# One convolution channel group on GpSimd, the last expert added by one-hot matmuls, and modulation columns made on chip

## The chip, the cores and the metric
The kernel runs on one core of a Trainium2 chip. The metric is the time of one execution in microseconds of the device, the median of several runs.

## What is computed
Two layers with shared weights over 384 tokens (128 context tokens, 256 latent tokens) of width 1024, all in float32.
```python
def trunk_layer(x, mod, n1, n2, w_in, ..., rope=None, ctx_kv=None):
    sh1, sc1, g1, sh2, sc2, g2 = [mod[:, i][:, None, :] for i in range(6)]
    h = rms_norm(x, n1) * (1.0 + sc1) + sh1
    proj = h @ w_in
    q, k, v, u = jnp.split(proj, [Q_W, Q_W + KV_W, Q_W + 2 * KV_W], axis=-1)
    ...
    attn = block_attention(q, k_all, v_all)
    conv = conv_module(u, dw_w, dw_b, ln_g, ln_b)   # 31 taps over 512 channels, depthwise
    x = x + g1 * (jnp.concatenate([attn, conv], axis=-1) @ w_out)
    h2 = rms_norm(x, n2) * (1.0 + sc2) + sh2
    x = x + g2 * grouped_moe(h2, ...)               # 16 experts, 2 for a token
    return x, k, v
```
The six modulation vectors of a layer are silu(c) @ w_mod + b_mod, one set for context and one for latent tokens.

## The kernel before
The tokens are three tiles of 128 rows, tile 0 the context, tiles 1 and 2 latent. Everything is written out by hand: each engine has its own instruction list and semaphores order them. SyncE (SP) issues the weight loads, each 2 MB into one of eight slots of a ring, in the order of use, as soon as the slot's last user is done.

**Columns.** Norm 1 is folded into transposes: TensorE (PE) multiplies x, as stationary, by a diagonal of the row factors (L1397, `scr` and `big` are SBUF areas, `ps` is PSUM), and ACT (L731) and DVE (L952) scale and shift the transposed tiles with per-channel columns `modcol` while copying them to `hT`. `vector` (L1343) makes a modulation vector by 16 matmuls; DVE's `mod_take` (L914, L923) adds the bias and multiplies by the norm's gain; `columns` (L388) writes the rows to DRAM and reads them back as columns. In layer 0 ACT issues this between its first work and the transposed tiles, in layer 1 POOL does it early in the expert stage. Vector 2 of layer 1 is computed right after the experts of layer 0.

**Convolution.** After the projections (L1327) the gated input is transposed to channels on partitions, `zT`, 4 groups of 128 channels. DVE applies tap after tap, for the 4 groups in turn (`tap`, L996 for the first, L1000 for the others: a scalar_tensor_tensor over 128 context or 256 latent columns, both tensor operands in SBUF). The 31 context taps come first. Of the 31 latent taps 6 lie around the rotary work of the three tiles (`rope`, L1031 to L1065), 4 late ones after it, and 3 in each of the first seven heads of the attention. In rope, POOL makes the norm factors (L543 to L546) from DVE's sums (L1031), and DVE waits for them at L1034. PE interleaves quarters of vector 3 with the transposes of the roped tiles (L1451). In each head PE does transposes (L1486) and scores (L1462), a piece of vector 4 (L1357) and the product with v; DVE does maxima (L1081), 3 taps and the output (L1089). In head 3 DVE also takes half of vector 4 (L918, L923) and needs `gainB`, which POOL loads (L564).

**Experts.** POOL gathers the token rows of a pair of experts (L604), PE transposes them (L1602), and per expert come gate and up (L1618), ACT's sigmoid (L873), two DVE products (L1299, L1301), two transposes (L1627), a DVE copy (L1305), and the down projection (L1634), which is issued one expert late: down of e - 1 after gate/up of e. More than 64 tokens for an expert are an overflow, run in a loop of its own. ACT copies each result (`take_y`, L840) and stores it to `expert_rows` in DRAM (L843). After the last store POOL gathers the two result rows of every token (L650), ACT scales one (L705), and DVE combines (`combine`, L933, L934, L935) into x. Layer 1 starts from there with the square sums (L709), POOL's factor (L514, L515) and the diagonal (L944).

The order of the loads at an expert stage's end, from the list `loads`:
```python
    for e in range(1, E):
        experts += [("g", l, e), ("u", l, e), ("d", l, e - 1)]
    return items, experts + [("d", l, E - 1)]
```


## Time and profile before
| | before |
|---|---|
| median of 3 runs | 1169.36 us (1165.12 to 1169.71) |
| profiled execution, its time | 1165.68 us |
| its span | 1163.8 us |
| PE busy, DVE, ACT, POOL | 980.0, 407.9, 158.2, 116.8 us |
| granted TensorE clock, mean | 0.92 of full speed |
| DMA | 331.71 MB, mean 285 GB/s |

Times in the trace run from the span's start. A busy PE is not PE at its peak. Every float32 matmul stands in the trace as two PE instructions. The profile's shares are averages over stages: what a change is worth is read where its instructions stand, from what waits last there.

### The profile page before, as it was taken

What the parts mean: (1) busy time and instruction counts of PE and PEld (TensorE: products, weight loads), DVE (VectorE), ACT (ScalarE), POOL (GpSimd) and SP (SyncE); (2) the same over time, 40 slices, a digit from 0 to 9 for tenths busy, and PEclk for the clock granted to TensorE, in tenths of its full rate; (3) what the DMA queues carried; (4) which work ended last, traced back from release to release, by engine and by line L of the source; (5) the groups of instructions that cost most, each with busy time, mean ns of one, the idle gap of its engine ahead of it and who ended that gap; (6) DMA issues with size and microseconds to landing.
All of it is one profiled execution on the core that took longest, in us unless ns stands there. A gap on an engine that the chain in (4) does not pass through costs nothing.

```text
span 1163.8 us, 11201 instructions
## 1 busy us (share of the span) xinstructions
PE 980.0 (84%) x4106; PEld 443.5 (38%) x4106; DVE 407.9 (35%) x1072; ACT 158.2 (14%) x362; POOL 116.8 (10%) x164
## 2 busy tenths in 40 slices
PE   3589979999889988997839996999858997978890
PEld 0344525545333333333225553554523333333330
DVE  0019868733411111111042986954421111111113
ACT  0110123311000000000021023431100000000001
POOL 0100310230110000000030030041010000000001
PEclk8789979998989999998869997999769999998996
DMA  9934992348999987999975434034965999999805
GB/s 315 378 135 144 218 387 116 145 127 305 425 412 422 422 367 261 396 426 425 411 296 185 144 139 192 8 139 162 346 249 207 409 426 424 425 419 426 372 19 180
DMA packets 65412, 331.71 MB, mean 285 GB/s; under 512 B 6993, under 2 KB 9713, under 8 KB 48929
## 3 DMA queue, kind: packets, MB, share of 16 engines
q1 hardware_dynamic: 44224, 277.89, 59.9%
q10 hardware_dynamic: 12464, 23.79, 6.9%
q0 software_dynamic: 8624, 28.71, 6.8%
q8 instruction: 62, 1.02, 0.4%
q14 instruction: 38, 0.30, 0.1%
HBM read 308.25 MB, written 22.12 MB: 284 GB/s over the span
## 4 chain that ended last, share of the span: by engine, by line
PE 64%; DMA 19%; DVE 10%; issue 2%; ACT 2%; SPq 2%; POOL 1%; ACTq 0%; DVEq 0%; POOLq 0%
PE ps L1618 19%; PE ps L1327 15%; DMA big<-in_w_up_dram 10%; PE ps L1634 9%; PE ps L1534 7%; DVE scr L1000 4%; PE ps L1343 4%; DMA x<-in_x_sample_dram 2%; DMA big<-in_w_down_dram 2%; PE ps L1462 2%; DMA scr<-h_rows,slot_tok 1%; PE ps L1397 1%; DMA scr<-expert_rows,pick_y 1%; PE ps L1357 1%; PE ps L1602 1%
## 5 line engine op out<-in xcount | busy, mean ns | idle before, releaser
L1618 PE MATMUL ps<-big 128*64 128x512 f32 x1024 | 246.9, 633 | 41.3 <-DMA big<-in_w_up_dram 23.1
L1000 DVE SCALAR_TENSOR_TENSOR scr<-scr,convw 128x128 f32<-128x128 f32 (+1 forms) x480 | 160.5, 408 | 0.0
L1618 PEld LDWEIGHTS ps<-big 128*64 128x64 f32 x1024 | 82.0, 145 | 181.5 <-issue 167.4
L1634 PE MATMUL ps<-big,scr 128*64 128x512 f32 x624 | 146.3, 605 | 5.0 <-DVE scr L1290 4.3
L1327 PE MATMUL ps<-big 128*128 128x512 f32 (+1 forms) x384 | 146.1, 541 | 0.0
L1299 DVE TENSOR_TENSOR scr<-ps,scr 128x256 f32<-128x256 f32 x32 | 13.6, 425 | 309.9 <-ACT scr L873 309.9
L1343 PE MATMUL ps<-big,cs_rep 128*64 128x512 f32 x320 | 83.3, 667 | 22.0 <-DMA big<-in_w_mod_dram 22.0
L1327 PEld LDWEIGHTS ps<-big 128*128 128x128 f32 x384 | 72.9, 191 | 69.8 <-issue 67.5
L1534 PE MATMUL ps<-big 128*128 128x512 f32 x192 | 84.4, 594 | 1.4 <-ACT big L739 1.4
L1634 PEld LDWEIGHTS ps<-big,scr 128*64 128x64 f32 x624 | 49.8, 139 | 88.8 <-issue 88.3
L873 ACT ACTIVATE scr<-ps 128x256 f32<-128x256 f32 x32 | 12.3, 384 | 356.6 <-PE ps L1618 356.6
L1618 PE MATMUL ps<-big,scr 128*64 128x512 f32 x224 | 51.3, 612 | 5.9 <-DVE scr L1279 5.9
L1534 PEld LDWEIGHTS ps<-big 128*128 128x128 f32 x192 | 35.7, 190 | 43.0 <-issue 41.1
L1343 PEld LDWEIGHTS ps<-big,cs_rep 128*64 128x64 f32 x320 | 23.5, 152 | 70.4 <-issue 51.6
L1397 PE MATMUL ps<-big,x 128*128 128x128 f32 x96 | 23.8, 427 | 31.2 <-DVE big L944 21.6
L604 POOL DMA_INDIRECT scr<-h_rows,slot_tok x16 | 15.5, 969 | 288.2 <-PE ps L1602 244.3
L1462 PE MATMUL ps<-scr 64*128 64x384 f32 (+1 forms) x96 | 39.4, 500 | 0.0
L1270 DVE COPY big<-ps 128x512 f32<-128x512 f32 x32 | 20.6, 686 | 50.5 <-PE ps L1602 50.5
L1397 PEld LDWEIGHTS ps<-big,x 128*128 128x128 f32 x96 | 23.2, 335 | 33.1 <-issue 33.1
L1486 PE MATMUL ps<-table_sb,scr 128*128 128x128 f32 x112 | 22.9, 307 | 15.0 <-ACT scr L795 15.0
L1357 PE MATMUL ps<-big,cs_rep 128*2 128x512 f32 x64 | 33.4, 649 | 0.0
L1327 PEld LDWEIGHTS ps<-scr 128*128 128x128 f32 x224 | 26.9, 196 | 16.0 <-issue 13.8
(198 smaller groups left out, 758.3 us busy)
## 6 DMA issues: line engine op xcount, KB each, us to landing
big<-in_w_gate_dram SPq DMA_DIRECT2D x32, 2048.0 KB, 15.5
big<-in_w_up_dram SPq DMA_DIRECT2D x32, 2048.0 KB, 20.6
big<-in_w_down_dram SPq DMA_DIRECT2D x32, 2048.0 KB, 18.0
big<-in_w_mod_dram SPq DMA_DIRECT2D x23, 2048.0 KB, 17.5
big<-in_w_in_dram SPq DMA_DIRECT2D x6, 2048.0 KB, 28.6
expert_rows<-scr ACTq DMA_DIRECT2D x78, 128.0 KB, 8.0
big<-in_w_out_dram SPq DMA_DIRECT2D x4, 2048.0 KB, 17.4
expert_rows<-x ACTq DMA_DIRECT2D x1, 6656.0 KB, 36.4
```

Of the source, the lines that this page charges most:

```text
L604: pool.indirect_dma_start(out=xs[:, i % 2, :], out_offset=None, in_=h2_dram, in_offset=bass.IndirectOffsetOnAxis(ap=slot_tok[:, i * NT:i * ...
L1000: v.scalar_tensor_tensor(out, span, w, out, ALU.mult, ALU.add).then_inc(conv_step[part_], 1)
L1270: ins = v.tensor_copy(hT[i % 2][:, 4 * b:4 * b + 4, :].rearrange("p k n -> p (k n)"), ps[:, XT + b, :])
L1327: mm = pe.matmul(out, stationary(k), moving(k), start=(k == 0), stop=(k == n - 1))
L1343: mm = pe.matmul(ps[lane * LP:(lane + 1) * LP, mod_bank(l, j), :], cs_rep[:, k, :], w[:, lane * LW:(lane + 1) * LW], start=(k == 0), stop= ...
L1357: mm = pe.matmul(ps[0:2, mod_bank(l, c), :], cs_rep[:, k, 0:2], slot_k(slot_of(n), b - a)[:, k - a, (c - 8) * SEG:(c - 7) * SEG], start=(k ...
L1397: mm = pe.matmul(ps[:, n % 4, m * P:(m + 1) * P], x[:, t, 4 * (n % 2) + m::KD], diag[:, t, :], start=True, stop=True)
L1462: pe.matmul(ps[:, 4 + t, 0:P * len(ks)], qT[g_ * HD:(g_ + 1) * HD, t, j * P:(j + 1) * P], kT[g_ * HD:(g_ + 1) * HD, ks[0] * P:(ks[-1] + 1) ...
L1486: mm = pe.transpose(ps[:, 1 + t, n * P:(n + 1) * P], prob[:, t, n * P:(n + 1) * P], ident)
L1534: mm = pe.matmul(ps[:, out_bank(t, n), :], hT[t][:, k, :], slot_w(s)[:, k, :], start=(k == 0), stop=(k == KD - 1))
L1618: mm = pe.matmul(ps[b * TT:(b + 1) * TT, bank, :].rearrange("p (m n) -> p m n", m=2), tokens(k), w[:, :, k, b * HF:(b + 1) * HF], start=(k ...
L1634: mm = pe.matmul(ps[b * TT:(b + 1) * TT, bank, :], src[:, k % 2 * P + k // 2 * TT:k % 2 * P + (k // 2 + 1) * TT], w[:, k, b * SEG:(b + 1) ...
```

## The change
It has three parts.

1. The convolution's last group of 128 channels goes to POOL, as a product and a sum per tap (the product buffers lie in `sg`); DVE keeps 3 groups. POOL does all 31 context taps before its first norm factor of rope, 3 latent taps before the second, 3 before the third, 6 after it, and 19 after the gate's round trip and before the load of `gainB`. PE's `conv_back` waits for both.
2. The columns are made on chip: rows go from PSUM to SBUF unchanged, 16 matmuls with `ident` turn each into 64 by 2 pieces, and DVE adds bias and gain that were loaded as columns. The start's loads put x before the second vector; x is transposed between the vectors for two tiles and after the first two projections for the third. The two broadcasts of the layer norm's parameters are issued later. Vector 2 of layer 1 moves behind that layer's projections.
3. Expert 15 is not stored and gathered. DVE makes marks of token against slot, weighted; PE transposes them and ACT keeps them. In the last expert, down of 14 and the overflow come ahead of gate/up. After down of 15, 6 matmuls of 64 rows spread its rows to tokens in PSUM, and DVE adds them (`add_last`) after the picked rows (`add_picked`). The gather waits for the stores up to expert 14.

```diff
+DVE_CM, POOL_M = CM - 1, CM - 1
+POOL_TAPS = [3, 3, 6]
-        items = vec[4:6] + proj + vec[6:10] + out + vec[10:12]
+        items = proj + vec[4:10] + out + vec[10:12]
...
             load_vector(0, 0)
-            load_vector(0, 1)
             sp.dma_start(x[:, 0, :], x_prompt[0]).then_inc(x_in, 16)
             sp.dma_start(x[:, 1:3, :], x_sample[0].rearrange("(t p) n -> p t n", p=P)).then_inc(x_in, 16)
+            load_vector(0, 1)
             for l in range(LAYERS):
-                if l:
-                    load_vector(l, 2)
...
+                    for k in range(k0, k0 + n):
+                        span = zT[:, POOL_M, k + o0:k + o0 + w_]
+                        w = convw[:, POOL_M, k:k + 1]
+                        product = sg[:, k % 2 * 2 * P:k % 2 * 2 * P + w_]
...
+                            done = l * (2 * TAPS) + part_ * TAPS + k
+                            pool.wait_ge(pool_conv, done - 1)
+                            g.tensor_scalar(product, span, w, None, ALU.mult).then_inc(pool_mul, 1)
+                            pool.wait_ge(pool_conv, done)
+                            pool.wait_ge(pool_mul, l * (2 * TAPS - 2) + part_ * (TAPS - 1) + k)
+                            g.tensor_tensor(out, out, product, ALU.add).then_inc(pool_conv, 1)
...
+                taps(0, 0, TAPS)
+                for t in range(TILES):
+                    if t == 1:
+                        pool.wait_ge(zT_ready, l * 3 + 3)
+                    if t:
+                        taps(1, sum(POOL_TAPS[:t - 1]), POOL_TAPS[t - 1])
                     pool.wait_ge(qk_ss, l * 3 + t + 1)
...
+                taps(1, sum(POOL_TAPS[:2]), POOL_TAPS[2])
                 pool.wait_ge(mod_taken, taken_at(l, 2))
                 lane_out(pool, mod_dram[:, 2 * D:3 * D], rowC, modC_st)
...
+                taps(1, sum(POOL_TAPS), TAPS - sum(POOL_TAPS))
                 pool.wait_ge(slot_used[slot_of(("in", l, 3))], uses(("in", l, 3)))
                 pool.dma_start(gainB, norm2_g[l:l + 1, :].broadcast_to([2, D])).then_inc(gain_in, 16)
...
                 for b in range(2):
-                    pool.wait_ge(y_st[b], (l + 1) * (E * 16))
+                    pool.wait_ge(y_st[b], (l + 1) * ((E // 2 - b) * 32))
...
+                soon = 1 if l + 1 < LAYERS else TILES
+                for t in range(soon):
+                    scale_pick(l, t)
                 take_y(E - 1)
-            for t in range(TILES):
-                scale_pick(LAYERS - 1, t)
+                for t in range(soon, TILES):
+                    scale_pick(l, t)
...
+            def add_last(l, t):
+
+                a1 = pick_buf[t][1]
+                dve.wait_ge(fin_ps, l * TILES + t + 1)
+                step.link(v.tensor_tensor(a1, ps[:, 2 * FIN[t]:2 * FIN[t] + 2, :].rearrange("p b n -> p (b n)"),
+                                          gateB[:, group(t), :], ALU.mult))
+                v.tensor_tensor(x[:, t, :], x[:, t, :], a1, ALU.add).then_inc(combined, 1)
...
                 if l:
-                    mod_take(l, 2)
-                    combine(l - 1, 0)
-                    combine(l - 1, 1)
+                    add_picked(l - 1, 0)
+                    add_last(l - 1, 0)
+                    columns(l)
+                    add_picked(l - 1, 1)
                     scale_tile(0)
-                    combine(l - 1, 2)
+                    add_last(l - 1, 1)
+                    add_picked(l - 1, 2)
+                    add_last(l - 1, 2)
...
+            def columns(l, s_):
+
+                pe.wait_ge(mod_taken, taken_at(l, s_))
+                for k in range(KD):
+                    for b in range(LANES):
+                        mm = pe.matmul(ps[b * LP:(b + 1) * LP, col_bank(l, s_), 2 * (s_ * KD + k):2 * (s_ * KD + k) + 2],
+                                       rowA[:, s_ * LW + k:(s_ + 1) * LW:KD], ident[:, b * LP:b * LP + 2],
+                                       start=True, stop=True)
+                mm.then_inc(cols_ps, 1)
...
+                    if e == E - 1:
+                        down_main(e - 1)
                     loaded(("g", l, e))
                     loaded(("u", l, e))
+                    if e == E - 1:
+                        overflow(pe, n, run, ov_at)
                     gate_up(GU, e, lambda k: hT[i % 2][:, k, j * TT:(j + 1) * TT]).then_inc(gu_ps, 1)
...
                 down_main(E - 1)
+                pe.wait_ge(y_taken, (l + 1) * E)
+                for t in range(TILES):
+                    for b in range(2):
+                        mm = pe.matmul(ps[:, 2 * FIN[t] + b, :], last_T[b * TT:(b + 1) * TT, t, :],
+                                       ybuf[b * TT:(b + 1) * TT, 1, :], start=True, stop=True)
+                    mm.then_inc(fin_ps, 1)
```

The order on POOL around rope, before (L543 to L546 are the norm factors of a tile, L551 and L553 the cache outputs, L292 to L285 the gate's way through DRAM, L564 the gain):
```order
L540 MEMSET scr 128x4x15
L543 TENSOR_SCALAR stat<-stat 128x8
...
L551 DMA out_dram<-scr 128x128
L553 DMA out_dram<-scr 128x128
L543 TENSOR_SCALAR stat<-stat 128x8
L544 TENSOR_SCALAR stat<-stat 128x2
L546 TENSOR_TENSOR stat<-stat 128x10
...
L519 DMA gateB<-mod_rows 128x2x1024
L285 DMA rowC<-in_b_mod_dram 64x512 x2
L564 DMA big<-in_norm_g_dram 2x1024
```
And now, from the cache outputs on (L559 is a product, L562 a sum, L574 to L577 the norm factors):
```order
L582 DMA out_dram<-scr 128x128
L584 DMA out_dram<-scr 128x128
L554 TENSOR_SCALAR scr<-scr,convw 128x256
L559 TENSOR_SCALAR scr<-scr,convw 128x256
L562 TENSOR_TENSOR scr<-scr 128x256
L559 TENSOR_SCALAR scr<-scr,convw 128x256
L562 TENSOR_TENSOR scr<-scr 128x256
L574 TENSOR_SCALAR stat<-stat 128x8
L575 TENSOR_SCALAR stat<-stat 128x2
L577 TENSOR_TENSOR stat<-stat 128x10
```
Between the outputs for the cache and the second tile's factors there now stand five operations on 256 columns; ahead of the first tile's stand 61 on 128.

The order on PE from the last down projection of layer 0 to the projections of layer 1, before:
```order
L1618 MATMUL ps<-big 64x512 x16
L1634 MATMUL ps<-big,scr 64x512 x8
L1627 MATMUL ps<-table_sb,scr 128x128 x2
...
L1648 MATMUL ps<-table_sb 1x1 x2
L1634 MATMUL ps<-big,scr 64x512 x8
L1343 MATMUL ps<-big,cs_rep 64x512 x16
L1397 MATMUL ps<-big,x 128x128 x24
L1327 MATMUL ps<-big 128x512 x24
```
And now (L1727 gate/up, L1743 down, L1830 the one-hot matmuls, L1462 the columns, L1472 the transposes of x, L1419 the projections):
```order
L1727 MATMUL ps<-big 64x512 x16
L1736 MATMUL ps<-table_sb,scr 128x128 x2
L1759 MATMUL ps<-table_sb 1x1 x2
L1743 MATMUL ps<-big,scr 64x512 x8
L1830 MATMUL ps<-scr 128x512 x6
L1462 MATMUL ps<-table_sb,scr 64x2 x32
L1472 MATMUL ps<-big,x 128x128 x16
L1419 MATMUL ps<-big 128x512 x16
L1472 MATMUL ps<-big,x 128x128 x8
L1419 MATMUL ps<-big 128x512 x8
```
The down projection of expert 14 has left its place between gate/up and down of 15, vector 2 (L1343) is gone from here, and two groups stand between the last down projection and the transposes of x.

## Rows read from the trace of the kernel before

**Rows 1.** Page, chain that ended last, shares by engine:
```profile
PE 64%; DMA 19%; DVE 10%; issue 2%; ACT 2%; SPq 2%; POOL 1%; ACTq 0%; DVEq 0%; POOLq 0%
```
**Rows 2.** Chain in order of time, the start: start us, us, what:
```profile
17.38 23.91 DMA x<-in_x_sample_dram
...
59.79 1.52 ACT big L731 x4
...
65.56 21.34 PE ps L1327 x48
```
**Rows 3.** Timeline of DVE in heads 1 and 2 (start, us, what, idle before):
```profile
181.39 4.83 DVE L1000 SCALAR_TENSOR_TENSOR scr<-scr,convw 128x256 f32<-128x256 f32 x12
...
187.59 0.56 DVE L1081 TENSOR_REDUCE stat<-ps 128x1 f32<-128x384 f32 x1 [0.23 <-PE ps L1462]
188.07 4.83 DVE L1000 SCALAR_TENSOR_TENSOR scr<-scr,convw 128x256 f32<-128x256 f32 x12
```
**Rows 4.** Timeline at the end of layer 0's experts, and windows, DMA GB/s last:
```profile
560.40 9.48 PE L1618 MATMUL ps<-big 128*64 128x512 f32 x32 [4.07 <-DMA big<-in_w_up_dram]
...
574.27 3.65 PE L1634 MATMUL ps<-big,scr 128*64 128x512 f32 x16 [0.35 <-DVE scr L1305]
...
560.00:565.00 5.00, 4.60 (x12) 1.65 (x14) 0.00 (x0) 0.00 (x0) 0.00 (x0) 0.50 1.01 421
```
**Rows 5.** Timeline from the experts of layer 0 to the projections of layer 1:
```profile
594.37 1.15 ACT L705 ACTIVATE scr<-scr,gates 128x1024 f32<-128x1024 f32 x1 [15.75 <-DMA scr<-expert_rows,pick_y]
...
604.37 11.72 PE L1397 MATMUL ps<-big,x 128*128 128x128 f32 x48 [19.07 <-DVE big L944]
...
615.92 1.45 PE L1327 MATMUL ps<-big 128*128 128x512 f32 x3
```
**Rows 6.** Timeline of the program's end:
```profile
1118.48 7.09 PE L1618 MATMUL ps<-big,scr 128*64 128x512 f32 x32 [0.78 <-DVE scr L1279]
...
1128.09 5.35 PE L1634 MATMUL ps<-big,scr 128*64 128x512 f32 x16 [0.61 <-DVE scr L1290]
...
1148.21 1.15 ACT L705 ACTIVATE scr<-scr,gates 128x1024 f32<-128x1024 f32 x1 [10.33 <-DMA scr<-expert_rows,pick_y]
...
1159.52 1.23 DVE L935 TENSOR_TENSOR x<-x,scr 128x1024 f32<-128x1024 f32 x1
```
**Rows 7.** Timeline of PE, last group of vector 3 in layer 0:
```profile
155.15 1.94 PE L1343 MATMUL ps<-big,cs_rep 128*64 128x512 f32 x8
```
**Rows 8.** Groups of POOL by form: busy us, mean ns, idle before:
```profile
L575 POOL TENSOR_TENSOR big<-big,lnB 128x512 f32<-128x512 f32 x6 | 7.6, 1263 | 5.5 <-DVE big L1102 5.5
...
L539 POOL MEMSET scr<- 128x120 f32 x2 | 0.5, 234 | 0.0
```
**Rows 9.** Timelines where DVE and POOL meet with SBUF operands:
```profile
240.45 1.28 POOL L580 TENSOR_TENSOR big<-big,scr 128x512 f32<-128x512 f32 x1 [0.80 <-ACT scr L818]
...
240.99 1.28 DVE L1138 TENSOR_TENSOR x<-x,scr 128x512 f32<-128x512 f32 x1
...
604.47 1.00 POOL L514 TENSOR_SCALAR stat<-stat 128x1 f32<-128x1 f32 x1 [0.57 <-ACT big L709]
...
609.20 0.19 POOL L514 TENSOR_SCALAR stat<-stat 128x1 f32<-128x1 f32 x1 [2.12 <-ACT big L709]
...
244.76 0.69 DVE L1138 TENSOR_TENSOR x<-x,scr 128x512 f32<-128x512 f32 x1
```
**Rows 10.** Timeline of rope in layer 0, small POOL operations beside taps:
```profile
124.55 1.65 DVE L1000 SCALAR_TENSOR_TENSOR scr<-scr,convw 128x256 f32<-128x256 f32 x4
...
125.55 2.11 POOL L546 TENSOR_TENSOR stat<-stat 128x10 f32<-128x10 f32 x1
```
**Rows 11.** Timelines of rope: POOL in layer 0, DVE's last step, PE in layer 1:
```profile
132.52 0.35 POOL L543 TENSOR_SCALAR stat<-stat 128x8 f32<-128x8 f32 x1 [1.52 <-DVE stat L1031]
...
149.90 0.28 DVE L1065 TENSOR_TENSOR scr<-scr 128x128 f32<-128x128 f32 x1
...
690.00 1.94 PE L1343 MATMUL ps<-big,cs_rep 128*64 128x512 f32 x8
...
699.41 0.28 DVE L1065 TENSOR_TENSOR scr<-scr 128x128 f32<-128x128 f32 x1
```

More of the change, by code:

```diff
@@ L171, in mod_bank, with col_bank @@
     if j == 2:
-        return 1 if l == 0 else 4
+        return 1
     return {3: 0, 8: 0, 9: 0, 5: 3}[j]
+def col_bank(l, s):
+    return 5 if l else 6 + s
+FIN = [0, 1, 3]
 def taken_at(l, j):
@@ L439, in _ @@
                     load(("in", l, m), w_in_v[l, :, :, c0:c0 + n], n)
-                for j in (2, 3, 4) if l == 0 else (3, 4):
+                for j in (2, 3, 4):
                     load_vector(l, j)
@@ L834, in take_y @@
                 def take_y(k):
[L836 removed]
+                    j = k % 2
+                    before = l * (E // 2 - j) + k // 2
                     if past(before):
@@ L975, in _ @@
                     mod_take(0, 1)
+                    columns(0)
+                dve.wait_ge(cols_ready, l + 1)
                 for t in range(TILES):
@@ L1296, in run @@
                         more_hidT()
+                    if e == E - 1:
+                        overflow(dve, n, run, ov_at)
                     dve.wait_ge(sig_ready, l * E + e + 1)
@@ L1363, in head_fill, with x_transposed @@
                             mm.then_inc(slot_used[slot_of(n)], 1)
+            def columns(l, s_):
[6 more added lines that the diff above has]
+                mm.then_inc(cols_ps, 1)
+            def x_transposed(l, t):
+                pe.wait_ge(diag_ready, l * 3 + t + 1)
+                for n in range(2 * t, 2 * t + 2):
+                    for m in range(4):
+                        mm = pe.matmul(ps[:, n % 4, m * P:(m + 1) * P], x[:, t, 4 * (n % 2) + m::KD], diag[:, t, :],
+                                       start=True, stop=True)
+                    mm.then_inc(hT_ps, 1)
             vector(0, 0)
-            vector(0, 1)
             pe.wait_ge(table_in, 16)
             pe.wait_ge(router_in, 32)
+            columns(0, 0)
+            x_transposed(0, 0)
+            x_transposed(0, 1)
+            vector(0, 1)
+            columns(0, 1)
             for l in range(LAYERS):
                 if l:
-                    vector(l, 2)
-                    pe.wait_ge(y_taken, l * E)
+                    columns(l, 0)
+                    columns(l, 1)
+                    x_transposed(l, 0)
+                    x_transposed(l, 1)
                 def transposed(t):
```

167 lines of the change are left out of this document (104 added, 63 removed).

## The prediction
> **What bounds the kernel now.** I read the page's chain of waits first, then the timeline of each stretch that the change touches, then the by-form groups for prices. The chain is mostly TensorE, with DVE in second place among the engines [rows 1]: what counts is whether a piece lies where TensorE waits. Four places matter.
>
> *The start.* x lands at 17.38 + 23.91 = 41.3 us, ACT applies the columns, after a round trip of the rows through DRAM, only at 59.79, and the first projection starts at 65.56 [rows 2]. *The attention stretch.* In heads 1 to 3 one DVE tap group follows another every 188.07 - 181.39 = 6.68 us, and DVE waits for PE in between, 0.23 before one of its reductions [rows 3]. So a head takes PE 6.68 us, and taking taps off DVE shortens no head; only the four late taps before head 0 stand alone on the path. *The end of layer 0.* PE waited for the last up-weights until 560.3, then came gate/up of expert 15 and down of 14, and down of 15 from 574.27 to 577.9 [rows 4]; the picked rows were there only at 594.37 and projections began at 615.92 [rows 5]. *The end of the program.* From the last down projection's copy to the picked rows 10.33 us, then three combines until 1159.52 + 1.23 = 1160.75 [rows 6].
>
> **Part 1, the start: gain 10.9 us.** The 9.5 MB before x's landing are the same; now the last to land is the last quarter of the second vector, at 41.3. Its 8 PE instructions take 2.7 us (0.33 each, between the 0.24 and the half-clock 0.43; an instruction of that kind is 1.94/8 = 0.24 [rows 7]), the DVE copy 0.8, which gives 44.8. Then the columns: 16 matmuls are 32 instructions, since each float32 matmul shows as two. Their stationary is strided like x's in the x transposes, which cost 11.72/48 = 0.244 each with 128 columns [rows 5]; with 64 columns I take half, 0.122, so 3.9 us (bounds: a quarter to all of 0.244, 2.0 to 7.8). Two small DVE operations, 0.5, and four activations, 1.5 [rows 2], give the first projection at 50.8, 14.8 earlier. The transposes of tile 2 are moved, not removed: they now stand between projections and cost 16 x 0.244 = 3.9. So 10.9 gained, between 7.0 and 12.8.
>
> **Part 2, the convolution's fourth channel group on POOL.** Removed from DVE per layer: 31 prompt and 31 sample operations. Added to POOL: 61 operations on 128 columns and 61 on 256 (a product and a sum for each tap, one for the first). POOL prices: a two-input sum of 512 columns is 1.263 [rows 8], one of almost no columns 0.19 [rows 9], so 2.1 ns a column: 0.73 for 256, 0.46 for 128. A one-input product of that width does not occur; it costs at least the 0.234 of a 120-column memset [rows 8] and at most the sum's 0.73. I take 0.45, in the middle. With 0.12 between operations a sample tap is 1.3 us (1.1 to 1.6), a prompt tap 0.88.
> The Trainium skill (GPSIMD Engine Reference, Performance versus the Vector engine) has 2.6 cycles an element for two inputs and (When to use GPSIMD) one-input operations near line rate; by it a product of 256 would be about 0.40 us, an estimate, and the sum would move by under 1 us. The same section says to leave elementwise work to the Vector engine.
>
> *The two engines block each other.* At 240.99 a DVE add of two SBUF operands, 0.69 elsewhere, took 1.28 because a POOL sum had begun at 240.45: it ended 0.54 after POOL's end, the time of its own data. At 604.47 a POOL operation of 0.19 took 1.00, until DVE's ended [rows 9]. A tap on DVE has two SBUF inputs too. POOL gets in between two back-to-back taps: at 124.55 four taps kept their pace, 1.65, while tiny POOL operations passed [rows 10]. So I let them alternate: one POOL operation, one DVE tap. A sample tap of POOL then takes 1.6 us and lets through 2 DVE taps, 0.8 each in place of 4.83/12 = 0.40 [rows 3].
> The Trainium skill (SBUF — State Buffer, Who interferes with whom) says whoever starts first holds the pair for the whole instruction. The POOL operation of 2.11 us with 10 columns left the DVE taps alone [rows 10], against the letter of that: I charge the reading time only. By the page's wording a DVE tap under POOL would be 1.0 us, and the total about 4 us more.
>
> Prompt taps: POOL needs 31 x 1.0 = 31 us blocked, DVE does 93 operations in about the 33 us that 124 took. No change. *Rope:* POOL now has 3 taps between its first and second norm. POOL has issued the cache DMAs at 132.52 - 1.52 = 131.0 and began the second norm at 132.5 [rows 11]; three taps of 1.3 and a little blocking last until 135.3: +2.8. Rope of tile 1, 4.4 us of two-input operations, meets 3 more taps: +2.0, minus 0.4 for the missing channel and the 0.4 that DVE waited: +4.0. Rope of tile 2 meets the 6 taps: +3.5. It ended at 150.18 in layer 0 and 699.69 in layer 1 [rows 11]; now 7.5 later. In layer 0 PE came to it 5 us after it was ready (its last vector group began at 155.15 [rows 7]), so +3.1 remain. In layer 1 PE waited for it, so all 7.5 count. *Late taps:* 12 for 16, -1.6. *Heads:* POOL has 19 taps left after the gate's DMA round trip. It starts them about 169, and between then and head 1's taps DVE is mostly idle; there 7 to 8 cost nothing. The other 11 to 12 fall on heads 1 and 2, where DVE's 9 taps take 7.2 at full alternation and the head 8.8 in place of 6.68: +2.1, and +1.4 in the second: +3.5. Nothing comes back in later heads, PE's 6.68 hold. Layer 0: 3.1 - 1.6 + 3.5 + 0.2 = +5.2. Layer 1: 7.5 - 1.6 + 3.5 = +9.4.
> *Queued behind POOL's taps:* the load of norm2's gain. DVE asks for it in head 3, at about 204 in this timeline; POOL is done by 192. Cover of 10 us.
>
> **Part 3, vector 2 of layer 1** moves out of the gap after the experts to behind the projections: 32 instructions of 0.22 (7.09/32, [rows 6]), 7.1 us. I cost it at nothing: PE would be ready for the last rope at 690.0 + 7.1 + 1.9 + two groups of 2.6 = 704.2 [rows 11], and the rope, covering it, is ready at 707.2. If rope is not late, 4 us. The PE wait of 3 us brings its low clock: 560.40 shows 9.48 for 32 instructions after a wait of 4.07 where 0.22 each is usual [rows 4, 6]. +1.0.
>
> **Part 4, expert 15 by one-hot matmuls, end of layer 0: loss 7.1 us.** Down of expert 14 must now come first, but its weights land after the up-weights of 15 (2 MB at 421 GB/s are 5.0 us [rows 4]): 565.3. Down 14 at part-low clock until 571.3, gate/up 15 until 578.5, its sigmoid and products are no longer covered (2.5, as between 1118.48 + 7.09 and 1128.09 [rows 6]), down 15 until 584.7 (before: 577.9). Row 14's copy ends at 571.9; at the 15.75 us that copy to picked row took [rows 5] the rows are there at 587.7. ACT scales tile 0 first, 1.15, then copies expert 15, 0.6: 589.5. 12 final PE instructions of 512 columns, 4.0 at half to full clock, then 64 column instructions, 7.8: 601.3. DVE waits for them with its list: columns 0.6, then 3.85 + 0.3 + 2.5 + 3.85 + 2.5 + 0.3 to the diagonal of tile 1, at 615.2 (operations of 1.23 [rows 6] and the gaps). Transposes 3.9 give the first projection at 619.1, with tile 2's 3.9 still to come: 623.0 against 615.92. Bounds: columns at 0.06 and 0.244 each, +2 to +15.
>
> **Part 5.** Nine more small DVE operations before the experts, 2 us, mostly behind the gather: +0.5. *End of program:* the picked rows come while PE does expert 15, so the three combines start about 1137.6 rather than 1149.5 (1148.21 and ACT's scaling), but they grow from 3.76 to 3.85 + 2.5 each; and expert 15's chain is 1.2 longer (2.5 uncovered, against 1.3 of the slow 5.35 down [rows 6]). Tile 2 is done at 1156.7, not 1160.75 [rows 6]: -4.0.
>
> **Sum:** -10.9 + 5.2 + 7.1 + 9.4 + 1.0 + 0.5 - 4.0 = +8.3, on the profiled execution's 1165.68: 1174.0. That run lies 3.7 below the median shown, 1169.36. I add half of it, 1.8: **1176 us**, slower by 0.6%.
>
> **Rivals.**
> *A. The block costs little* (POOL slips into DVE's bubbles, products are short). For: tiny POOL operations did not slow taps [rows 10]. Against: both 512-column cases were blocked in full. Layer 0 gains 1.9, layer 1 loses 2.4 (vector 2 is then exposed): -10.9 - 1.9 + 7.1 + 2.4 + 0.5 - 4.0 = -6.8, on the same base 1161: faster.
> *B. POOL becomes the bound.* At over 1.9 us a blocked tap the 19 taps are not done when DVE asks for the gain in head 3, and everything behind stands. At 2.3 us: 8 us a layer there and 3 more in rope: 1176 + 22 = 1198. For: rope and taps of DVE block POOL too [rows 9]; against: the prices above leave 10 us.
> *C. The chip-made columns of layer 1 are dear:* PE at low clock through final and column matmuls, 0.244 each: +8, 1184.
> *D. The change does not unload DVE in effect but the start and the end pay as computed and layer 0's end costs only its lower bound:* 1171, no change.
>
> **Chances.** My forecast 0.52, of which 0.24 slower, 0.23 within, 0.05 faster, since its terms sit near the line of 0.5% (5.8 us, about what a measurement of this kernel tells from no change). A 0.27 (0.25 faster), B 0.11, C 0.05, D 0.05. Faster 0.30, same 0.27, slower 0.43. Range 1156 to 1196: from A with the start's best bound to B nearly whole.
>
> **What would show it.** The first projection near 51 us. DVE taps of 256 columns at 0.7 to 0.9 wherever POOL taps run, 0.40 else; POOL sums of 0.73 stretched to about 1.0. Rope of tile 2 ending 7 us later relative to the projections; heads 1 and 2 near 8.8 us, heads 4 to 7 at 6.68. At layer 0's end: down 14 waiting for weights, DVE waiting for the columns about 7 us. I am wrong if taps keep 0.40 beside POOL taps, if a head past 2 still waits for POOL, or if the projections of layer 1 begin no later than before relative to the last up-weights.

## The result, and the profile after

The changed kernel takes **1192.1 us** (median of 4 runs, 1183.5 to 1193.8) where the kernel before takes 1167.2 (median of 4 beside it): **ratio 1.020, 95% interval 1.017 to 1.024**, slower by 24.9 us. The forecast was 1176 us, slower by 0.6%. The direction was as forecast and the time lies in the range of 1156 to 1196; the loss is three times the 8.3 us that the sum gave, and not the forecast case came but rival B, in which POOL becomes the bound. The profiled execution of the changed kernel took 1190.67 us, its span 1188.8.

The table is read from the traces: when TensorE begins or ends each stage in the two profiled executions, and the lead (-) or lag (+) of the changed kernel. The filler matmuls are the piece of vector 4 in a head (L1357 before, L1449 now); "convolution transposed back" is the start of the transposes that bring the convolution's result back behind the last head.

| place (TensorE) | before | after | after - before |
|---|---|---|---|
| first projection of layer 0 | 65.4 | 46.7 | -18.7 |
| its projections done | 140.6 | 126.6 | -14.0 |
| filler matmuls of head 0 | 172.3 | 164.4 | -7.9 |
| convolution transposed back | 222.2 | 224.2 | +2.0 |
| first gate/up | 316.4 | 317.9 | +1.5 |
| last down projection's weights land | 570.8 | 577.0 | +6.2 |
| layer 1's projections done | 690.1 | 699.0 | +9.0 |
| filler matmuls of head 0 | 717.6 | 737.2 | +19.7 |
| convolution transposed back | 767.9 | 797.1 | +29.3 |
| last down projection's weights land | 1105.0 | 1129.6 | +24.6 |
| end of the span | 1163.8 | 1188.8 | +25.0 |

The losses stand between "projections done" and "convolution transposed back", 16.0 us in layer 0 and 20.3 in layer 1. The chain of waits, which had 1% of POOL [rows 1], now goes through POOL's taps. The page, shares by engine (this chain goes back no further than 706.84 us, so its shares add up to 40%):

```profile
PE 23%; DMA 7%; POOL 4%; DVE 3%; issue 2%; ACT 1%; ACTq 0%; DVEq 0%; SPq 0%; POOLq 0%
```

*The start.* The timeline of TensorE in the changed kernel (start, us, then engine, line, operation, tiles, shape, count, and in brackets the idle time before and what ended it), to be held against [rows 2]:

```profile
34.71 7.09 PE L1435 MATMUL ps<-big,cs_rep 128*64 128x512 f32 x32
42.59 2.09 PE L1462 MATMUL ps<-table_sb,scr 128*64 128x2 f32 x32 [0.79 <-DVE scr L958]
46.70 15.70 PE L1419 MATMUL ps<-big 128*128 128x512 f32 x32 [2.02 <-ACT big L762]
62.23 3.84 PE L1472 MATMUL ps<-big,x 128*128 128x128 f32 x16
```

The 32 column instructions take 2.09 us, 0.065 each; the first projection starts at 46.70, and tile 2's transposes (3.84) stand between projections as computed.

*POOL's prices.* Groups of the changed kernel by form (busy us, mean ns, idle before); before, only a sum of 512 columns and tiny operations were to be seen [rows 8]:

```profile
L559 POOL TENSOR_SCALAR scr<-scr,convw 128x256 f32<-128x256 f32 x60 | 67.7, 1129 | 0.1
L562 POOL TENSOR_TENSOR scr<-scr 128x256 f32<-128x256 f32 x60 | 44.3, 738 | 9.2 <-POOL scr L559 0.8
L559 POOL TENSOR_SCALAR scr<-scr,convw 128x128 f32<-128x128 f32 x60 | 38.5, 641 | 0.0
L562 POOL TENSOR_TENSOR scr<-scr 128x128 f32<-128x128 f32 x60 | 33.8, 563 | 9.3 <-POOL scr L559 0.5
L554 POOL TENSOR_SCALAR scr<-scr,convw 128x256 f32<-128x256 f32 x2 | 1.1, 564 | 0.1
```

The sums cost what was forecast. The product (L559) is the dear half of the tap, dearer than the sum, though it reads one tensor; the first tap (L554), which multiplies and adds, takes half of it. With no tap of DVE beside it (first three rows below, timeline of POOL) one tap follows the other every 1.77 us; beside DVE's taps (the next three) 1.95. DVE's taps there (last row, timeline of DVE) take 3.97/6 = 0.66 each, where 0.40 was usual [rows 3]:

```profile
162.93 0.92 POOL L559 TENSOR_SCALAR scr<-scr,convw 128x256 f32<-128x256 f32 x1
164.00 0.72 POOL L562 TENSOR_TENSOR scr<-scr 128x256 f32<-128x256 f32 x1
164.70 0.92 POOL L559 TENSOR_SCALAR scr<-scr,convw 128x256 f32<-128x256 f32 x1
...
183.39 1.09 POOL L559 TENSOR_SCALAR scr<-scr,convw 128x256 f32<-128x256 f32 x1
184.64 0.72 POOL L562 TENSOR_TENSOR scr<-scr 128x256 f32<-128x256 f32 x1
185.34 1.10 POOL L559 TENSOR_SCALAR scr<-scr,convw 128x256 f32<-128x256 f32 x1
...
181.67 3.97 DVE L1076 SCALAR_TENSOR_TENSOR scr<-scr,convw 128x256 f32<-128x256 f32 x6
```

*Rope.* The timeline of DVE shows it waiting for POOL's norm factors three times, and its own two-input steps stretched (L1127 takes 1.23; the same step, L1051 before, took 0.82 and 0.83):

```profile
118.50 0.83 DVE L1110 TENSOR_TENSOR scr<-scr,stat 128x640 f32<-128x640 f32 x1 [7.72 <-POOL stat L577]
...
128.86 0.83 DVE L1110 TENSOR_TENSOR scr<-scr,stat 128x640 f32<-128x640 f32 x1 [5.11 <-POOL stat L577]
...
140.15 0.83 DVE L1110 TENSOR_TENSOR scr<-scr,stat 128x640 f32<-128x640 f32 x1 [1.88 <-POOL stat L577]
...
142.01 1.23 DVE L1127 TENSOR_TENSOR scr<-scr,table_sb 128x640 f32<-128x640 f32 x1
...
145.49 0.28 DVE L1141 TENSOR_TENSOR scr<-scr 128x128 f32<-128x128 f32 x1
```

The first wait, 7.72, is for POOL's 31 prompt taps: they ran from 75.00 to 115.83, 1.32 us each. Rope ends at 145.77, which is 159.7 in the timeline of before (its projections ended 14.0 later), against 150.19 [rows 11]: 9.5 later.

*The heads.* One head of each layer takes 15.6 and 14.8 us where the others take 6.7 to 8.1. In the timeline around it, DVE wants the gain at 193.1; POOL is at its taps until 196.7 and only then issues the load. The first row is the same DVE step in the kernel before, which did not wait:

```profile
200.28 0.68 DVE L923 SCALAR_TENSOR_TENSOR big<-big 2x512 f32<-2x512 f32 x1
...
192.46 0.67 DVE L966 TENSOR_TENSOR big<-ps,big 2x512 f32<-2x512 f32 x1
...
196.01 0.72 POOL L562 TENSOR_TENSOR scr<-scr 128x256 f32<-128x256 f32 x1
196.67 0.58 POOL L597 DMA_DIRECT2D big<-in_norm_g_dram  x1
198.69 0.68 DVE L971 SCALAR_TENSOR_TENSOR big<-big 2x512 f32<-2x512 f32 x1 [5.56 <-DMA big<-in_norm_g_dram]
```

TensorE falls idle behind it, and when it comes back its granted clock is low. Windows (length; busy time of PE, PEld, DVE, ACT, POOL with counts; granted clock; DMA share; GB/s):

```profile
200.00:209.00 9.00, 9.00 (x28) 5.65 (x29) 5.79 (x17) 3.83 (x13) 0.00 (x0) 0.50 0.00 0
216.00:222.00 6.00, 6.00 (x30) 2.82 (x29) 4.56 (x12) 2.95 (x10) 0.00 (x0) 1.00 0.44 177
```

After DVE's wait of 5.6 us TensorE runs the next 9 us at 0.50, the level of 1.2 GHz. The head takes 15.65 us instead of 6.68 and the next one 7.65, so the wait costs nearly twice its length.

*The end of layer 0* (timeline of TensorE; [rows 4, 5] before): down of 14 waits for weights, and the columns come before the first transposes.

```profile
572.29 5.50 PE L1743 MATMUL ps<-big,scr 128*64 128x512 f32 x16 [8.10 <-DMA big<-in_w_down_dram]
577.61 7.05 PE L1727 MATMUL ps<-big 128*64 128x512 f32 x32
...
587.07 3.65 PE L1743 MATMUL ps<-big,scr 128*64 128x512 f32 x16 [0.35 <-DVE scr L1394]
594.31 5.49 PE L1830 MATMUL ps<-scr 64*128 64x512 f32 x12 [3.59 <-ACT scr L875]
599.73 4.01 PE L1462 MATMUL ps<-table_sb,scr 128*64 128x2 f32 x64
```

### The profile page after: what moved, and what is told of

The parts are those of the page before. It is cut to its first block and busy times, and to the rows that moved or that the text cites. A ratio compares the mean times of both kernels' runs of the same rounds, so it can differ in the third digit from the quotient of the medians.

```text
span 1188.8 us, 11788 instructions
## 1 busy us (share of the span) xinstructions
PE 1013.0 (85%) x4264; PEld 464.4 (39%) x4264; DVE 419.7 (35%) x982; ACT 158.8 (13%) x364; POOL 297.0 (25%) x404
## 5 line engine op out<-in xcount | busy, mean ns | idle before, releaser
L1727 PE MATMUL ps<-big 128*64 128x512 f32 x1024 | 243.0, 625 | 31.4 <-issue 12.3
L1743 PE MATMUL ps<-big,scr 128*64 128x512 f32 x624 | 151.4, 624 | 13.1 <-DMA big<-in_w_down_dram 8.1
L1076 DVE SCALAR_TENSOR_TENSOR scr<-scr,convw 128x128 f32<-128x128 f32 (+1 forms) x360 | 150.4, 488 | 0.0
L1419 PE MATMUL ps<-big 128*128 128x512 f32 (+1 forms) x384 | 147.4, 544 | 2.0 <-ACT big L762 2.0
L1727 PEld LDWEIGHTS ps<-big 128*64 128x64 f32 x1024 | 80.7, 143 | 168.9 <-issue 156.7
L559 POOL TENSOR_SCALAR scr<-scr,convw 128x128 f32<-128x128 f32 (+1 forms) x120 | 106.2, 885 | 0.1
L1419 PEld LDWEIGHTS ps<-big 128*128 128x128 f32 x384 | 73.0, 192 | 71.6 <-issue 67.1
L639 POOL DMA_INDIRECT scr<-h_rows,slot_tok x16 | 15.4, 964 | 311.3 <-PE ps L1711 265.0
L1743 PEld LDWEIGHTS ps<-big,scr 128*64 128x64 f32 x624 | 51.2, 143 | 99.7 <-issue 97.6
L562 POOL TENSOR_TENSOR scr<-scr 128x128 f32<-128x128 f32 (+1 forms) x120 | 78.0, 650 | 18.5 <-POOL scr L559 1.3
L1727 PE MATMUL ps<-big,scr 128*64 128x512 f32 x224 | 51.3, 612 | 5.9 <-DVE scr L1366 5.9
L1570 PE MATMUL ps<-scr 64*128 64x384 f32 (+1 forms) x96 | 42.9, 539 | 0.0
L659 POOL DMA_INDIRECT scr<-h_rows,slot_tok x7 | 6.6, 948 | 131.3 <-PE ps L1727 126.2
L1419 PE MATMUL ps<-scr 128*128 128x64 f32 x224 | 31.3, 297 | 8.8 <-DVE big L1164 8.8
L1419 PEld LDWEIGHTS ps<-scr 128*128 128x128 f32 x224 | 29.0, 209 | 24.1 <-issue 13.5
L1357 DVE COPY big<-ps 128x512 f32<-128x512 f32 x32 | 20.6, 686 | 46.4 <-PE ps L1711 46.4
## 6 DMA issues: line engine op xcount, KB each, us to landing
big<-in_w_gate_dram SPq DMA_DIRECT2D x32, 2048.0 KB, 14.6
big<-in_w_up_dram SPq DMA_DIRECT2D x32, 2048.0 KB, 20.3
```

What stands on the lines that cost most here:

```text
L559: g.tensor_scalar(product, span, w, None, ALU.mult).then_inc(pool_mul, 1)
L562: g.tensor_tensor(out, out, product, ALU.add).then_inc(pool_conv, 1)
L639: pool.indirect_dma_start(out=xs[:, i % 2, :], out_offset=None, in_=h2_dram, in_offset=bass.IndirectOffsetOnAxis(ap=slot_tok[:, i * NT:i * ...
L1076: v.scalar_tensor_tensor(out, span, w, out, ALU.mult, ALU.add).then_inc(conv_step[part_], 1)
L1357: ins = v.tensor_copy(hT[i % 2][:, 4 * b:4 * b + 4, :].rearrange("p k n -> p (k n)"), ps[:, XT + b, :])
L1419: mm = pe.matmul(out, stationary(k), moving(k), start=(k == 0), stop=(k == n - 1))
```

## The experiments

Ten runs of nine kernels follow (e11 is e5's kernel again); "e" names are labels. All ratios are to the kernel before, each to the executions of it that ran beside. My theory after reading the traces was a queue: POOL's taps hold back what stands behind them (norm factors, the gain load). The rival was the port: DVE and POOL slow each other wherever the taps stand.

**e1, the gain load ahead of the taps.**
```diff
-                taps(1, sum(POOL_TAPS), TAPS - sum(POOL_TAPS))
                 pool.wait_ge(slot_used[slot_of(("in", l, 3))], uses(("in", l, 3)))
                 pool.dma_start(gainB, norm2_g[l:l + 1, :].broadcast_to([2, D])).then_inc(gain_in, 16)
+                taps(1, sum(POOL_TAPS), TAPS - sum(POOL_TAPS))
```


> The load of norm2's gain is issued ahead of POOL's last 19 taps instead of behind them. Theory (the queue): in the changed kernel one head of each layer takes 15.6 us instead of 6.7 because DVE waits for that gain, which sits behind POOL's taps. With the load ahead, all heads from the third on take 6.7 us, each layer's attention ends about 9.8 us sooner, and the whole is 1172 us (-19.6). Rival (the port): it is the DVE and POOL taps blocking each other that makes the heads long; then the heads stay long and the whole moves by less than 4 us.

Measured 1176.8 us (ratio 1.010, 1.008 to 1.012): 15.3 us below the changed kernel. The waits of DVE in layer 0's heads no longer have the gain among them; the changed kernel's first, then e1's (total, times, longest):
```profile
DVE big L971 <- DMA big<-in_norm_g_dram: 5.6, 1, 5.6
```
```profile
DVE stat L1156 <- PE ps L1570: 9.4, 9, 2.1
DVE stat L1162 <- PE ps L1419: 6.4, 2, 6.1
DVE big L966 <- PE ps L1449: 1.5, 1, 1.5
```
From projections done to the convolution transposed back, layer 1 is 9.5 us shorter, as expected. Layer 0 is only 4.5 shorter: there TensorE did heads 0 and 1 at the low clock for longer (12.4 and 8.2 us, where the changed kernel took 7.7 and 6.7; granted clock 0.50 to 0.51 from 160 to 180, where the changed kernel had 0.86 from 165 to 170 and then 1.00). That is not the edit's doing: one execution of e5's kernel has the same slow heads (12.4 and 8.1), another of the same kernel, in e11, has 9.0 and 6.7. So some 5 us of this stretch change from execution to execution, and the profiled one of e1 had them. The queue theory holds; the port rival does not explain the long head.

**e2, the whole convolution on DVE.**
```diff
-DVE_CM, POOL_M = CM - 1, CM - 1
+DVE_CM = CM
...
-                taps(0, 0, TAPS)
...
-                        pe.wait_ge(pool_conv, (l + 1) * (2 * TAPS))
```


> The fourth channel group of the convolution goes back to DVE; the columns made on chip, vector 2 behind the projections and the one-hot matmuls stay, and the gain load stays where it is in the program (nothing long is ahead of it now). Theory: the whole of the loss in the attention stretch comes from POOL's taps: the gain wait 2 x 9.8, the later rope and the late taps 6.1 in layer 0 and about 6.5 in layer 1 (vector 2, 7.1 us of PE, then stands partly uncovered): 1160 us, below the kernel before. Rival: the taps on POOL cost only the wait for the gain, and taking a channel group off DVE is otherwise worth its price: then the time equals that of the run with the load ahead, about 1172 us.

Measured 1162.6 us (ratio 0.996, 0.994 to 0.998): in this kernel all POOL taps together cost 29.5 us, and without them the change is slightly faster than the kernel before. From projections done to the convolution transposed back: 81.8 in each layer; before 81.6 and 77.8, after 97.6 and 98.1. So POOL's group costs 16 us in each layer. The 4.0 that layer 1 keeps is vector 2, no longer covered.

**e3, no POOL taps between the norms of rope** (on e1).
```diff
-POOL_TAPS = [3, 3, 6]
+POOL_TAPS = [0, 0, 12]
```


> As the run with the gain load ahead, and in addition POOL does none of its sample taps between the three norms of rope: 12 stand behind the third norm instead of 3, 3 and 6. Theory (POOL holds the norm factors back behind its taps): rope of tile 2 ends about 7 us sooner in each layer; 4 us of that reach the heads in layer 0, and 4 in layer 1, where vector 2 then limits: 8 us below the run with the gain load ahead, about 1164 us. Rival (port): rope is slow because POOL's taps run beside it wherever they stand; then the late taps and rope just trade places and the time is within 3 us of that run.

Measured 1168.1 us (ratio 1.001, 0.999 to 1.004), 8.7 below e1, against 8 expected. From projections done to the first filler matmuls both layers are shorter, by 5.1 and 5.5 us. The scores of head 0 start at 144.4 instead of 149.9, and in layer 1 at 704.9 instead of 719.0 (of that, 6.5 is carried over from layer 0). Order on POOL, not only the port, made rope late. The first norm still waits, since the prompt taps still stand ahead of it:
```profile
119.83 0.82 DVE L1110 TENSOR_TENSOR scr<-scr,stat 128x640 f32<-128x640 f32 x1 [7.73 <-POOL stat L577]
```

**e4, the product in another form** (on e1).
```diff
-                            g.tensor_scalar(product, span, w, None, ALU.mult).then_inc(pool_mul, 1)
+                            g.tensor_scalar(product, span, w, zT[:, POOL_M, 0:1], ALU.mult, ALU.add).then_inc(pool_mul, 1)
```


> As the run with the gain load ahead, with the product of each POOL tap in the form of the first tap: two scalars from memory, multiply and add (the second scalar is a zero of the pad). In the changed kernel a product of 256 columns takes 0.92 us with nothing beside it, a first tap of two scalars only 0.57. If the form makes the difference, products fall to about 0.57 at 256 columns, rope of tile 2 ends 2 us sooner and the whole falls by 2 to 4 us against the run with the gain load ahead. If it is not the form (the first tap is short for another reason), the products stay at 0.92 or more and the time stays within 1.5 us.

Measured 1169.5 us (ratio 1.003, 1.001 to 1.005), 7.3 below e1: more than the 2 to 4 expected. It is the form. From projections done to the first filler matmuls layer 0 is 3.1 and layer 1 is 3.0 us shorter. The timeline of POOL with no tap of DVE beside it:
```profile
163.09 0.56 POOL L559 TENSOR_SCALAR scr<-scr,convw 128x256 f32<-128x256 f32 x1
163.80 0.72 POOL L562 TENSOR_TENSOR scr<-scr 128x256 f32<-128x256 f32 x1
164.51 0.56 POOL L559 TENSOR_SCALAR scr<-scr,convw 128x256 f32<-128x256 f32 x1
```
The same product, with a zero added, takes 0.56 instead of 0.92, and a tap 1.42 instead of 1.77.

**e5, expert 15 back to the gathered rows** (on e2).
```diff
-                    if e == E - 1:
-                        down_main(e - 1)
...
-                    if 0 < e < E - 1:
+                    if e:
                         down_main(e - 1)
...
-                        mm = pe.matmul(ps[:, 2 * FIN[t] + b, :], last_T[b * TT:(b + 1) * TT, t, :],
-                                       ybuf[b * TT:(b + 1) * TT, 1, :], start=True, stop=True)
...
-                add_last(l - 1, 0)
```


> On top of the run with the whole convolution on DVE (1162.6 us): expert 15 goes back to the gathered rows, down of 14 behind gate/up of 15, no one-hot matmuls, no marks; the columns stay on chip and now run while PE waits for the picked rows. Theory from the traces: the one-hot order costs 6.2 us at the last down projection of layer 0 and gives back about 3 by the shorter path to the first projection, and it gives about 2 us at the program's end. Undone: layer 0's last down 6 us sooner after its weights land, projections of layer 1 done 3 us sooner, program's end 2 us longer: 1161 us. Rival (the terms as forecast: 7.1 lost in layer 0, 4.0 gained at the end): 3.1 us less, 1159.5 us; second rival, that the order of the last experts makes no difference because picked rows set both ends: no change, 1162.6 within 1.5.

Measured 1155.6 us (ratio 0.989, 0.984 to 0.994), 7.0 below e2: more than either expectation; by the second measurement of the same kernel (e11, 1158.0) it is 4.6. In both kernels the last down projection's weights land at 565.6. The timeline of e2, then of e5, around that last down projection:
```profile
560.67 5.33 PE L1713 MATMUL ps<-big,scr 128*64 128x512 f32 x16 [8.28 <-DMA big<-in_w_down_dram]
565.82 7.05 PE L1697 MATMUL ps<-big 128*64 128x512 f32 x32
...
575.28 3.65 PE L1713 MATMUL ps<-big,scr 128*64 128x512 f32 x16 [0.35 <-DVE scr L1365]
```
```profile
562.54 3.62 PE L1673 MATMUL ps<-big,scr 128*64 128x512 f32 x16
...
567.11 3.65 PE L1673 MATMUL ps<-big,scr 128*64 128x512 f32 x16 [0.35 <-DVE scr L1327]
```
The reordering costs 8.2 us there, and 8.4 are left when layer 1's projections are done: nothing of it comes back. Nor does the program's end give anything in this pair: from the first gate/up of layer 1 to the end of the span e2 takes 308.1 and e5 308.3. Two other pairs below (e10, and e8 with e9) do not bear that out.

**e7, vector 2 of layer 1 back in front of the projections** (on e5).
```diff
-        items = proj + vec[4:10] + out + vec[10:12]
+        items = vec[4:6] + proj + vec[6:10] + out + vec[10:12]
...
                     columns(l, 1)
+                    vector(l, 2)
```


> As the run without one-hot matmuls, with vector 2 of layer 1 back in front of the projections, behind the columns. What is left of the change is the columns made on chip and the earlier transposes. Against the kernel before the start then gives 14 to 15 us up to the first expert. Theory: in the experts of layer 0 that lead shrinks to about 5 us, as it did in the run with the convolution on DVE, so the whole gains 5 to 7 us against before (1160 us), and against the run without one-hot matmuls vector 2 is hidden again: 2 to 4 us. Rival: the lead is kept when nothing else is changed, 1152 us.

Measured 1159.1 us (ratio 0.993, 0.989 to 0.996), near the 1160 expected, but not 2 to 4 us below e5, from which it can't be told apart. Two effects in the traces cancel. The attention stretch of layer 1 is 4.3 us shorter (76.5 against 80.8): vector 2 is covered again. But its 4 MB are now loaded while the picked rows are fetched. The row that shows the first rows arriving, in e5 and in e7, both timelines of ACT:
```profile
584.49 1.15 ACT L712 ACTIVATE big<-big,gates 128x1024 f32<-128x1024 f32 x1 [13.04 <-DMA scr<-expert_rows,pick_y]
```
```profile
584.62 1.15 ACT L715 ACTIVATE big<-big,gates 128x1024 f32<-128x1024 f32 x1 [17.15 <-DMA scr<-expert_rows,pick_y]
```
e7's last down projection ended 4 us sooner, and the rows came no sooner: 9.8 us from the gather's issue to arrival with the queues at 390 to 406 GB/s, 6.5 in e5, where they had gone down to 43 when it was issued. The start alone gives 14.6 us until the convolution is taken back (207.6 against 222.2) and about 8 in the time of the kernel.

**e8 and e9, the channel group kept on POOL with the repairs together**, e8 with the one-hot matmuls, e9 without: e1, e3 and e4 (and e5) in one.

> The change with three repairs together: the gain load ahead of POOL's last 19 taps, no POOL taps between the norms of rope, products in the two-scalar form. The three alone or in pairs gave 1168.1 and 1169.5 us. If they add up, rope of tile 2 ends as in the run with the convolution on DVE and no head waits: 1161 to 1163 us, no better than with the convolution on DVE (1162.6), since PE and not DVE sets the length of a head. Rival: freed DVE time is worth something somewhere (late taps 1.6 us a layer), then up to 3 us below the run with the convolution on DVE.

> All repairs that keep the channel group on POOL: gain load ahead, no taps between the norms, two-scalar products, and expert 15 back to the gathered rows. If the costs add, it is the 1162.5 us of the run with the three repairs less 7: 1155.5 us, equal to the run with the convolution on DVE and no one-hot matmuls. Rival: POOL's group costs a few us once nothing else hides it (vector 2 and rope limit layer 1): 1158 us or more.

Measured: e8 1162.5 us (ratio 0.996, 0.993 to 0.999), the same as e2. e9 1159.4 (0.993, 0.991 to 0.996), against 1155.6 and 1158.0 for e5's kernel: no gain over the convolution on DVE. Put right, POOL's taps cost and bring nothing that these runs can tell (e8 against e2 0.0 us; e9 against e11, measured beside it, 1.4 us with overlapping intervals), since TensorE's 6.7 us set a head. From e8 to e9 the gathered rows gave 3.1 us and not 7: layer 0's end became 7.1 shorter (from the landing of the last weights to projections done, 121.8 to 114.7), but the stretch from layer 1's first gate/up to the end 9.0 longer (302.5 to 311.5).

**e10, the changed kernel with only the one-hot order undone.**

> The changed kernel with only the one-hot order of expert 15 undone (POOL's taps, the late gain load and everything else stay). With the convolution on DVE the same edit gave 7.0 us, of which 8.4 at the end of layer 0 and nothing at the program's end. If that cost is independent of POOL's taps the changed kernel falls by 7 us to 1185. Rival: it depends on them, since in the changed kernel layer 0's experts start later and the weights may land before PE asks; then less than 3 us.

Measured 1185.9 us (ratio 1.016, 1.012 to 1.020), 6.2 below the changed kernel. That is near the 7 of independent costs, but the intervals of the two kernels overlap, as they do for e2 and e5's kernel and for e8 and e9: the one-hot order costs 3 to 7 us, the same way in all three pairs, and how it depends on POOL's taps is not resolved. In the traces layer 0's end is 4.0 shorter here (122.0 to 118.0), and from layer 1's first gate/up to the end it is 3.2 longer (305.7 to 308.9).

**e11, e5's kernel again.**

> The run with the convolution on DVE and no one-hot matmuls again, with five rounds, as the candidate that beats both kernels: 1156 us, a ratio of 0.990 to the kernel before; if the first measurement (1155.6, four runs) was lucky, up to 1159.

Measured 1158.0 us (ratio 0.993, 0.990 to 0.995). With the first measurement: 9 to 11 us faster than before, 34 to 37 than the changed kernel. No version beat it.

## Why the prediction was right and wrong

**Part 2, the price of a POOL tap: the step that failed.** "I take 0.45, in the middle" for a product of 256 columns, with 0.73 as the most: it is 0.92, above the bound. The bound leaned on a product costing "at most the sum's 0.73", and this form of product costs more than the sum. A tap was therefore 1.77 free and 1.95 blocked, not 1.3 and 1.6; e4, where the product takes 0.56, gives 7.3 us back by that alone. The price of the sum (0.73) and the direction were right. That POOL and DVE delay each other was right too, with other sizes: three DVE taps pass in one POOL tap, at 0.66 each, where I had two at 0.8. The effects below followed, and e2 measures them all at 29.5 us where my terms for the attention stretch gave 5.2 + 9.4:
- *The queue behind the taps.* "Cover of 10 us" for the gain load. In the timeline of before POOL would be done at 196.7 + 14.0 = 210.7 instead of 192, and DVE asked at 207 (forecast 204). Five us of the 18.7 between are an error of my own sum: from 169, 7.5 taps at 1.3 and 11.5 at 1.6 end at 197 and not at 192, so the cover was 7 us and not 10. The rest is mostly the price, which acts twice: the 19 taps took 35.6 us, 1.87 each, and they began only at 161.1 + 14.0 = 175.1, since the six taps ahead of the gate's round trip had taken 12.7 us. Rival B gave exactly this mechanism, from 1.9 us a blocked tap; 1.95 was measured. I put 0.11 on it and priced it at 8 us a layer; e1 measured 15.3 in all. I had not charged the 9 us at half clock behind the wait, which nearly double it.
- *"No change" for the prompt taps.* The 31 taps took 40.8 us, not 31, and DVE waited 7.72 for the first norm factor behind them.
- *Rope* ended 9.5 later in layer 0, where I had 7.5; DVE's waits for the second and third norm were as described, and e3 got back 8.7 by order alone. The slow heads 1 and 2 that I charged with 3.5 a layer did not happen: 7.7 and 6.7 us.

**Part 1, the start.** Forecast 10.9, measured 14.0 at the end of the projections. Columns cost 0.065 an instruction, near the lower bound of 0.06 that comes from a quarter of 0.244, not 0.122; whether the 2 moving or the 64 stationary columns set that is not shown. The second vector was done at 41.8, not at 44.0. What failed is the step after it: I carried the gain in full to the end of the program. In e2 the lead is 15.0 us at the first gate/up and 5.2 when layer 0's last weights land. In e5 it is 7.8 (its slow heads) and again 5.2, in e11 11.7 and 5.5. Three leads end at one landing time, 565.4 to 565.6, so it is not TensorE's start that sets it, but most likely the stream of weights; no run tests that.

**Part 3.** "At nothing" was covered only while rope was late, as the text says: with rope in order (e5 against e7) vector 2 costs 4 us in layer 1, the 4 that I had named for that case. That moving its loads away leaves the picked rows a free queue, worth about as much, was not foreseen.

**Part 4, layer 0's end.** Forecast +7.1, measured +2.8 from the landing of the last weights (9.0 - 6.2). The reordered experts came as computed: down 15 ended 590.72 - 6.2 = 584.5 in before's timeline, forecast 584.7. The columns were over-sized (4.0 against 7.8), the one-hot matmuls under-sized (5.5 against 4.0). But one-hot matmuls and on-chip columns were summed as one edit. Apart they are 8.4 lost (e2 against e5) and, with vector 2 moved away, about 5 gained: from the last weights' landing to projections done, before takes 119.3, e5 114.6.

**Part 5, the program's end.** Forecast -4.0. From the overflow part of expert 14 to the end the changed kernel is 2.9 us shorter, since 1163.8 - 1090.5 = 73.3 became 1188.8 - 1118.4 = 70.4. But from the landing of the last weights it is 58.8 before and 59.2 after. Ahead of expert 14's gate/up TensorE stood 2.7 us with nothing released that the profile shows and 1.8 us for weights, and the gate/up took 10.0 us instead of 7.1. So the term was partly right in its own stretch and brought nothing here. Whether the one-hot order pays at the end stays open: from layer 1's first gate/up to the end it is 0.2, 3.2 and 9.0 us shorter with it in the three pairs.

**The sum as a whole.** Without POOL's terms my parts give -10.9 + 7.1 + 0.5 - 4.0, and +4 for the vector 2 that then shows: -3.3. e2 came out 4.0 below the kernel before. That agreement is luck: the start was worth 5.2 and not 10.9 by layer 0's last weights, layer 0's end cost 3.7 and not 7.1, and the program's end gave nothing. Two figures do not follow from the prediction's own parts: its cases add up to 0.30 for "same" and 0.40 for "slower", not 0.27 and 0.43, and rival A with the start's best bound is 1159, not 1156.

**Not in the sum.** In all eleven profiles that start in the new way (columns on chip) TensorE stands 5.2 to 6.7 us between expert 0's gate/up and the next one in layer 0, with nothing released that the profile shows. In the kernel before it stands 0.55 there and 3.27 one expert later. The kernel before, the changed kernel, then e11, timelines of TensorE:
```profile
325.34 0.24 PE L1648 MATMUL ps<-table_sb 128*1 128x1 f32 x4
326.13 2.68 PE L1618 MATMUL ps<-big 128*64 128x512 f32 x6 [0.55 <-issue]
```
```profile
326.79 0.19 PE L1759 MATMUL ps<-table_sb 128*1 128x1 f32 x2
332.46 0.19 PE L1759 MATMUL ps<-table_sb 128*1 128x1 f32 x2 [5.48 <-issue]
```
```profile
313.57 0.24 PE L1687 MATMUL ps<-table_sb 128*1 128x1 f32 x4
319.20 6.11 PE L1657 MATMUL ps<-big 128*64 128x512 f32 x14 [5.40 <-issue]
```
With the one-hot order it stands in the middle of four short instructions that belong together, without it right behind them: undoing that order moves the wait and does not remove it. Until layer 0's last weights such waits of over 1 us add up to 3.3 us before and 8.2 in the changed kernel, about the 4.7 us that are lost between the first gate/up (+1.5) and the last weights (+6.2). Over the whole program they are 9.4 us before, 22.0 in the changed kernel, 19 to 21 in the other kernels with the one-hot order and 12 to 15 without it. Waiting for its program is the likely cause: a transfer of the instruction queue (16 KB, 1.07 us) began at 330.13, 2.3 us before TensorE went on, and every one of the 65 such waits in the twelve profiles ends 2.2 to 3.2 us after the start of one. No run changes the length of the program or its order alone, so that is not shown.

The mechanisms were named nearly all; the likeliest case was wrong because one price taken "in the middle" of two far rows decided between my forecast and rival B, and the point from which B decides was only 0.3 us above the 1.6 that I had.

## What to carry to other kernels

Before work is put on a helping engine, list what stands behind it in that engine's queue and move it ahead: here two small moves (the load ahead, taps behind the norms) were worth 24 us (changed kernel to e3), as much as the whole change had lost. Here the freed time of DVE, which waits for TensorE in the heads, was worth nothing, so the best case of this move was zero (e8 equals e2). And a lead must be followed to the end: 15 us gained before the experts were 5 behind them, where in three profiles with leads of 7.8 to 15.0 us the last weights landed at the same time.

## What the runs showed of the hardware that I had not expected

- **A product with one scalar is slower on POOL than the same product with a zero added:** 0.92 against 0.56 us at 256 columns, 0.60 against 0.45 at 128 (shortest of each in the traces of the changed kernel and e4). Per column that is 2.5 against 0.9 ns. The Trainium skill (GPSIMD Engine Reference, When to use GPSIMD) calls one-input operations on this engine roughly line-rate; the two-scalar form agrees, the one-scalar form (2.5 ns a column, slower than the two-input sum's 2.1) does not, and here the measurement decides.
- **A short wait cost TensorE nearly double.** DVE's 5.6 us of waiting were followed by 9 us of TensorE at the granted clock of 0.50, then 1.00 again (216 to 222).
- **The same kernel gets its clock back at different times.** In e5's profile TensorE is busy at 0.50 from 155 to 170 and has 1.00 from 175; in e11's, the same kernel, it has 1.00 from 165. The first two heads differ by 4.8 us for that (12.4 + 8.1 against 9.0 + 6.7).
- **The two engines share unevenly.** In e1 a DVE tap that started with a POOL sum (178.68) took 1.00 us, where the tap before it took 0.47, and the sum kept its 0.72; beside a product it is the product that stretches, 1.09 for 0.92. The Trainium skill (SBUF — State Buffer, Who interferes with whom) says that a Vector instruction with two SBUF inputs contends with a GpSimd instruction that reads SBUF; the tap of 1.00 agrees. The mean over six such taps of the changed kernel is 0.66, since not each starts with a sum.
- **A matmul with two columns of moving data** and a stationary of 64 strided columns costs 0.063 to 0.065 us an instruction (4.01/64 and 2.09/32 in the changed kernel).
